# A decoder layer with a mixture of experts: the overflow turns run ahead of the last static expert, whose rows are added by 0/1 products on TensorE

## The reference, cut to what matters

```python
h2 = rms_norm(x, norm2_g) * (1 + sc2) + sh2
# 4 groups of 8 experts; per token: best group, then the best 2 experts in it, with gates
hg = einsum('nd,edf->nef', h2, w_gate)      # 32 experts, d = 1024, f = 128
hu = einsum('nd,edf->nef', h2, w_up)
act = silu(hg) * hu * gates
x = x + gt2 * einsum('nef,efd->nd', act, w_down)
out = rms_norm(x, final_g)
```

## Time and profile before

| | us |
|---|---|
| median of 3 runs | 873.32 |
| lowest, highest | 872.92, 874.47 |
| the profiled execution, its device time | 874.96 |
| the same execution, span of the profile | 873.2 |
| granted TensorE clock, mean of the span | 0.983 of full |
| PE busy | 815.8 |
| DVE busy | 460.3 |
| POOL busy | 278.8 |
| ACT busy | 240.4 |

### The profile page before, as it was taken

How to read it: one execution, slowest core, us unless ns; L and a number is a source line. 1 busy time by engine, 2 the same in 40 slices (tenths; PEclk the granted TensorE clock), 3 DMA queues, 4 the chain that set the end, 5 groups by cost and what they waited for, 6 DMA issues and landing times. The chain is left out here.

```text
span 873.2 us, 17369 instructions
## 1 busy us (share of the span) xinstructions
PE 815.8 (93%) x7175; PEld 544.7 (62%) x7175; DVE 460.3 (53%) x1154; ACT 240.4 (28%) x581; POOL 278.8 (32%) x267
## 2 busy tenths in 40 slices
PE   8999999999999999799888999999999999999950
PEld 8557544544444355777777455555788888888830
DVE  3750478887830136467664244434645555454534
ACT  6220111112200143455543112221233223232214
POOL 5810000000499501452741100000135565543332
PEclk9999999999999999999999999999999999999995
DMA  9934433445111123000000881112889989888639
GB/s 315 324 90 135 145 120 121 139 158 172 37 38 36 27 70 133 18 3 4 4 4 20 308 325 48 49 73 96 325 296 301 303 285 273 277 267 261 206 73 367
DMA packets 79719, 136.35 MB, mean 156 GB/s; under 512 B 17213, under 2 KB 51226, under 8 KB 79642
## 3 DMA queue, kind: packets, MB, share of 16 engines
q1 hardware_dynamic: 69338, 118.44, 39.0%
q0 software_dynamic: 10304, 16.82, 8.2%
HBM read 124.18 MB, written 29.92 MB: 176 GB/s over the span
## 5 line engine op out<-in xcount | busy, mean ns | idle before, releaser
L792 PE MATMUL banks<-REG_W 128*128 128x512 f32 (+2 forms) x832 | 274.6, 499 | 0.9 <-DVE pend L1988 0.5
L792 PEld LDWEIGHTS banks<-REG_W 128*128 128x128 f32 (+1 forms) x832 | 125.9, 182 | 135.3 <-issue 133.8
L792 PE MATMUL banks<-REG_W,REG_Y 128*128 128x512 f32 x256 | 118.3, 599 | 1.4 <-DVE REG_Y L2236 1.1
L1434 ACT ACTIVATE REG_P<-banks 128x256 f32<-128x256 f32 (+2 forms) x126 | 53.5, 463 | 156.8 <-PE banks L792 137.7
L792 PE MATMUL banks<-REG_P 64*64 64x64 f32 (+3 forms) x2752 | 79.5, 230 | 13.1 <-issue 8.9
L792 PEld LDWEIGHTS banks<-REG_P 64*64 64x64 f32 (+1 forms) x2752 | 67.6, 135 | 23.0 <-issue 16.4
L1434 ACT ACTIVATE REG_Y<-banks,mod,s 128x128 f32<-128x128 f32 x136 | 51.2, 457 | 85.8 <-PE banks L1386 85.8
L792 PEld LDWEIGHTS banks<-REG_W,REG_Y 128*128 128x128 f32 x256 | 45.6, 191 | 44.3 <-issue 44.2
L792 PEld LDWEIGHTS banks<-REG_Y,REG_P 128*128 128x128 f32 (+1 forms) x616 | 63.1, 181 | 7.0 <-issue 7.0
L792 PE MATMUL banks<-REG_Y,REG_P 128*128 128x128 f32 (+1 forms) x616 | 66.6, 276 | 0.1
L636 POOL TENSOR_TENSOR REG_P<-REG_P 128x1040 f32<-128x1040 f32 x2 | 4.8, 2390 | 175.8 <-DVE REG_P L1801 175.8
(11 more groups left out here) (295 smaller groups left out, 1108.1 us busy)
## 6 DMA issues: line engine op xcount, KB each, us to landing
REG_P<-in_w_ada SPq DMA_DIRECT2D x20, 1024.0 KB, 6.2
REG_W<-in_w_in SPq DMA_DIRECT2D x17, 512.0 KB
REG_P<-in_moe_w_gate SPq DMA_DIRECT2D x17, 512.0 KB, 8.3
REG_W<-in_moe_w_gate SPq DMA_DIRECT2D x16, 512.0 KB, 6.4
REG_W<-in_moe_w_up SPq DMA_DIRECT2D x16, 512.0 KB, 10.7
REG_W<-in_moe_w_down SPq DMA_DIRECT2D x16, 512.0 KB, 16.7
REG_P<-in_moe_w_up SPq DMA_DIRECT2D x14, 512.0 KB, 14.9
REG_P<-in_moe_w_down SPq DMA_DIRECT2D x12, 512.0 KB, 21.2
```

The costliest lines, as they stand in the source:

```text
L792: return pe.matmul(o_, l, r, start=start, stop=stop, skip_group_check=True)
L1434: return act.activation(o_, i_, f, **kw)
```

## The change

The last static expert (turn 31, `LAST`) is taken out of the static loop and put behind the overflow loop on PE, ACT and DVE. The overflow turns take the counts from LAST on, and scatter from buffer `yo[2]`. POOL scatters no rows for turn 31; it gathers tile E+1 ahead of the scatter of turn 30. DVE builds, between the result of turn 30 and the overflow loop, 8 matrices `hot[:, j]` of 0 and 1 (partition = place in the expert's list, column = token of tile j). SP loads `y_d` to `x1` when the last overflow scatter has landed, without turn 31. PE then makes `hot[:, j]` transposed times `yo`, two `mm` calls of 128x512 for each tile j, into a pair of PSUM banks, and DVE adds the pair to the loaded tile (`completed(j)`); ACT squares the tile behind that. `xg[3]` is set to zero by POOL once before its first gather.

```diff
--- before.py
+++ after.py
@@ -261,6 +261,9 @@
             rt[name], o = area(REG_P, o, *shape)
         assert o == RT + RT_LEN
         fsq, _ = area(REG_W, 0, 2, D)
+        hot, _ = area(REG_W, SLOT, NT, P)
+        LAST = E - 1
+        assert LAST % RING == 9 and LAST % RES == 1
 
 
         ident = sb("ident", [P, P])
@@ -367,7 +370,7 @@
                  "rt_pos  rt_hot far_ld rt_ld rt_n "
                  " m_tx m_xa m_xd m_gu m_th m_act m_dn m_yd "
                  "ov_w "
-                 "rt_c rt_e1 rt_e2 rt_oh f_go ov_go st_x1 f_ss f_o").split()
+                 "rt_c rt_e1 rt_e2 rt_oh ov_go st_x1 f_ss f_o").split()
         s = {n: sem(n) for n in names}
         s_ada = [sem(f"ld_ada{i}") for i in range(4)]
         s_win = [sem(f"ld_win{i}") for i in range(2)]
@@ -539,7 +542,7 @@
                 e = sp.value_load(eid_view(i), min_val=0, max_val=E - 1)
                 load_expert(0, e, s["ov_w"])
 
-            sp.wait_ge(s["f_go"], 1)
+            sp.wait_ge(s["ov_go"], n_ov + 1)
 
             for j in range(NT):
                 sp.dma_start(x1[:, j], y_d[j * P:(j + 1) * P, :]).then_inc(s_w[j], 16)
@@ -739,8 +742,9 @@
             for e in range(2):
                 gather(TURN[e], e)
             gp.wait_ge(s["st_x1"], 16 * NT)
-            for e in range(2, BUF):
-                gather(TURN[e], e)
+            gather(TURN[2], 2)
+            ch.step(gp.memset(xg[3], 0.0))
+            gather(TURN[3], 3)
 
             def gather_behind(e):
                 if e + BUF < E:
@@ -749,13 +753,13 @@
 
             for e in range(3):
                 gather_behind(e)
-            for e in range(E):
+            for e in range(LAST):
+                if e == LAST - 1:
+                    gp.wait_ge(s["m_tx"], E + 1)
+                    gather(E + 1, 0)
                 gp.wait_ge(s["m_yd"], e + 1)
                 scatter_add(rows_of(TURN[e], 0), e % RES)
                 gather_behind(e + 3)
-                if e == E - 1:
-                    gp.wait_ge(s["m_tx"], E + 1)
-                    gather(E + 1, 0)
                 if e + BUF == E:
                     gp.wait_ge(s["far_ld"], 32)
                     gp.wait_ge(s["m_tx"], E - BUF + 1)
@@ -769,16 +773,15 @@
                     gp.sem_inc(s["ov_go"], 1)
             n_ov = gp.value_load(idy[0:1, 0:1], min_val=1, max_val=OVT)
             for b in range(RES):
-                gp.wait_ge(s_sc[b], 16 * len(range(b, E, RES)))
+                gp.wait_ge(s_sc[b], 16 * len(range(b, LAST, RES)))
             with gp.Fori(0, n_ov) as i:
                 ch.enter(i, 4)
-                scatter_add(rows_of(i + E, 1, i + (E + 1)), 0)
+                scatter_add(rows_of(i + E, 1, i + E), 2)
                 gp.wait_ge(s_gx[0], i * 16 + 16 * (E // BUF + 2))
                 at = rows_of(i + (E + 2), 0, count=i + (E + 2), done="m_tx")
                 fetch(at, 0)
-                gp.wait_ge(s_sc[0], i * 16 + 16 * (len(range(0, E, RES)) + 1))
+                gp.wait_ge(s_sc[2], i * 16 + 16 * (len(range(2, LAST, RES)) + 1))
                 gp.sem_inc(s["ov_go"], 1)
-            gp.sem_inc(s["f_go"], 1)
 
             for i in range(NT // 2):
                 gp.wait_ge(s["f_ss"], i + 1)
@@ -1411,21 +1414,36 @@
             ex_t(1, 1, 16)
             ex_gu(0, 0, 0, wsem=s_w[0], wcount=w_loads(0, 1), wait_free=False)
 
-            for e in range(1, E):
-                if e + 1 < E:
-                    ex_t(e + 1, (e + 1) % BUF, 16 * ((e + 1) // BUF + 1))
+            for e in range(1, LAST):
+                ex_t(e + 1, (e + 1) % BUF, 16 * ((e + 1) // BUF + 1))
                 ex_gu(e, e % 2, e % RING, wsem=s_w[e % RING], wcount=w_loads(e % RING, e // RING + 1), wait_free=e >= 2)
                 ex_dn(e - 1, (e - 1) % 2, (e - 1) % RING, wait_free=e >= 3)
             ex_t(E, 0, 16 * (E // BUF + 1))
-            ex_dn(E - 1, (E - 1) % 2, (E - 1) % RING)
+            ex_dn(LAST - 1, 0, (LAST - 1) % RING)
 
             pe.wait_ge(s["rt_n"], 1)
             n_ov = pe.value_load(idy[0:1, 0:1], min_val=1, max_val=OVT)
             with pe.Fori(0, n_ov) as i:
                 ex_gu(i + E, 0, 0, "m_", s["ov_w"], i * 48 + 48, False)
-                pe.wait_ge(s["m_yd"], i + E)
-                ex_dn(i + E, 0, 0, "m_", False)
                 ex_t(i + (E + 1), 0, i * 16 + 16 * (E // BUF + 2))
+                pe.wait_ge(s["m_yd"], i + LAST)
+                ex_dn(i + LAST, 0, 0, "m_", False)
+
+            ex_gu(LAST, 1, LAST % RING, wsem=s_w[LAST % RING], wcount=w_loads(LAST % RING, LAST // RING + 1), wait_free=False)
+            ex_dn(n_ov + LAST, 1, LAST % RING, wait_free=False)
+            beside(8, 2)
+            for j in range(NT):
+                q = 2 * ((j + 1) % 4)
+                if j == 3:
+                    pe.wait_ge(s["m_xa"], n_ov + (E + 1))
+                    pe.wait_ge(s["m_xd"], n_ov + (E + 1))
+                if j >= 4:
+                    pe.wait_ge(s["op_x1"], NT + j - 3)
+                for h in range(2):
+                    if j == 0:
+                        pe.wait_ge(s["m_yd"], n_ov + (E + h))
+                    last = mm(PS[q + h][:, :], hot[:, j, :], yo[LAST % RES][:, h * 512:(h + 1) * 512])
+                last.then_inc(s["op_ps"], 1)
 
 
         @block.scalar
@@ -1670,20 +1688,20 @@
 
             act.wait_ge(s["op_ps"], NT)
             modulated(xt[:, 0], 0, 1, "m_tx", "m_xa", 0)
-            for e in range(E):
-                if e + 1 < E:
-                    modulated(xt[:, (e + 1) % 2], 0, e + 2, "m_tx", "m_xa", 0)
+            for e in range(LAST):
+                modulated(xt[:, (e + 1) % 2], 0, e + 2, "m_tx", "m_xa", 0)
                 hidden(e, e % 2, free=e >= 2)
             modulated(xt[:, 0], 0, E + 1, "m_tx", "m_xa", 0)
             act.wait_ge(s["rt_n"], 1)
             n_ov = act.value_load(idy[0:1, 0:1], min_val=1, max_val=OVT)
             with act.Fori(0, n_ov) as i:
-                hidden(i + E, 0, free=False)
+                hidden(i + LAST, 0, free=False)
                 modulated(xt[:, 0], 0, i + (E + 2), "m_tx", "m_xa", 0)
+            hidden(n_ov + LAST, 1, free=False)
 
 
             for j in range(NT):
-                act.wait_ge(s_w[j], w_loads(j, len(range(j, E, RING))) + 16)
+                act.wait_ge(s["op_x1"], NT + j + 1)
                 if j >= 2:
                     act.wait_ge(s["ss_ready"], 2 * NT + j - 1)
                 fn(fsq[:, j % 2], x1[:, j], ACT.Square, scale=ROOT, accum_out=ss[:, 2, j:j + 1]).then_inc(s["ss_ready"], 1)
@@ -2235,35 +2253,57 @@
                     dve.wait_ge(s[pre + "dn"], e - 1)
                 stt(ac[:, par, :], a1[:, par, :], 0.5, PS[2 + par][:, P:2 * P], ALU.mult, ALU.mult).then_inc(s[pre + "act"], 1)
 
+            def scaled_halves(b, par, by):
+                return [stt(yo[b][:, h * 512:(h + 1) * 512], PS[4 + 2 * par + h][:, :], by, gtb[:, 1, h * 512:(h + 1) * 512],
+                            ALU.mult, ALU.mult) for h in range(2)]
+
             def result(e, par, pre="m_"):
-                b = e % RES if isinstance(e, int) else 0
+                b = e % RES
                 dve.wait_ge(s[pre + "dn"], e + 1)
-                if isinstance(e, int) and e >= RES:
+                if e >= RES:
                     dve.wait_ge(s_sc[b], 16 * (e // RES))
-                for h in range(2):
-                    last = stt(yo[b][:, h * 512:(h + 1) * 512], PS[4 + 2 * par + h][:, :], gate(TURN[e] if isinstance(e, int) else e), gtb[:, 1, h * 512:(h + 1) * 512],
-                               ALU.mult, ALU.mult)
-                last.then_inc(s[pre + "yd"], 1)
+                scaled_halves(b, par, gate(TURN[e]))[1].then_inc(s[pre + "yd"], 1)
 
             modulated(xt[:, 0], 1, "m_tx", "m_xd", 1)
-            for e in range(E):
-                if e + 1 < E:
-                    modulated(xt[:, (e + 1) % 2], e + 2, "m_tx", "m_xd", 1)
+            for e in range(LAST):
+                modulated(xt[:, (e + 1) % 2], e + 2, "m_tx", "m_xd", 1)
                 hidden(e, e % 2, free=e >= 2)
                 if e == 3:
                     dve.wait_ge(s["st_x1"], 16 * NT)
                 if e >= 1:
                     result(e - 1, (e - 1) % 2)
             modulated(xt[:, 0], E + 1, "m_tx", "m_xd", 1)
-            result(E - 1, (E - 1) % 2)
+            result(LAST - 1, 0)
+
+            ch.step(dve.tensor_copy(gap[:, 0:1], tbl[:, TURN[LAST], 0:1]))
+            ch.step(stt(left[:, :], i32[:, 0:NT], -float(P), gap[:, 0:1].to_broadcast([P, NT]), ALU.mult, ALU.add))
+            for j in range(NT):
+                ts(hot[:, j, :].rearrange("p (a b) -> p a b", a=KD), i128[:, :].rearrange("p (b a) -> p a b", a=KD), left[:, j:j + 1], None, ALU.is_equal)
             dve.wait_ge(s["far_ld"], 32)
             n_ov = dve.value_load(idy[0:1, 0:1], min_val=1, max_val=OVT)
             with dve.Fori(0, n_ov) as i:
                 ch.enter(i, 1)
-                hidden(i + E, 0, free=False)
```

(30 more changed lines are left out.)

## The result

| | before | after |
|---|---|---|
| median of 5 runs, us | 872.92 | 880.55 |
| lowest, highest | 870.51, 874.47 | 878.46, 881.62 |
| profiled execution: device time, span | 874.96, 873.2 | 880.62, 878.2 |
| granted TensorE clock, mean of the span | 0.983 | 0.988 |
| PE busy, DVE busy, POOL busy | 815.8, 460.3, 278.8 | 831.7, 472.8, 275.2 |

The kernel is slower by 0.87% (ratio 1.0087, 95% interval 1.0065 to 1.011), which is 7.6 us; +7.1 was forecast.

The account below looks back on a forecast made before the run. From 826 us on it saw a chain of handovers, with DVE deciding the tail. Terms 0 + 1.0 + 0 + 6.1 = +7.1 us on the median 873.3 gave 880.4 us, range 876.5 to 886.0.

Parts of the forecast that it names:

- Part 1: Moving turn 31 behind the overflow turn: gains 0, as the overflow gather lands when it did; bounds -0.2 to +2.4 us.
- The feared loss: Next gather, issued later behind turn 29's scatter, could make the overflow's down product 2.4 us late; taken as 0.
- Part 2: PE's new idle stretch before the overflow transposes: granted clock falls and slows the work behind; +1.0 us, bounds 0 and 2.5.
- Part 3: Turn 31 and the 0/1 products on PE behind the overflow turn: just in time, pacing up to tile 3; 0 us.
- Part 4: DVE in the tail: four adds, roots and a stall move the last scaling's end by +6.1 us; bounds +4.8, +8.3.
- The roots: POOL's roots in the tail: 0.73 us beside adds, so no stall there; without the rule the forecast is 1.4 us later.
- Rival A: PE's wait for the overflow gather: the overflow turn moves forward up to 5.5 us, giving 873.9 us; chance 6%.
- Rival B: Clock stays at 0.50 through the overflow's products, which take 7.5 instead of 3.8 us, giving 885.6 us; chance 8%.
- Rival C: Tail: the loads are the chain, so DVE's four extra adds vanish in waits, giving 876.3 us; chance 5%.
- What it said would show it wrong: Signs against it: the overflow's products start before 833, or DVE has gaps over 2 us in the tail.
- the window of 849 to 852: Start of the tail: the first load of `y_d` was expected at 849 to 852 us.

Follow-up runs that it names:

- c2: Kernel before in its old order, with turn 31's rows added by the 0/1 products in the tail and not scattered: 879.07 us, ratio 1.0074.
- a3: Changed kernel with turn 31's gate and up products put back into PE's wait for the overflow gather: 879.27 us, ratio 1.0079.
- d1: Changed kernel with the overflow weights released after turn 23 and final_g loaded behind them, gathers unchanged: 880.75 us, ratio 1.0092.
- d2: d1 with 20 matmul calls (40 small matmuls) added in PE's wait for the overflow gather: 878.65 us, ratio 1.0059.
- a2: Changed kernel with DVE's adds of tiles 4 to 7 cut from 1024 to 128 columns: 878.51 us, ratio 1.006.
- a6: Changed kernel with root_args(3) moved between the two scalings of pair 2, so the last root runs beside a scaling: 879.37 us, ratio 1.0081.
- a7: Changed kernel with the edits of a5 and a6 together: 876.08 us, ratio 1.0045.
- a4: Changed kernel with both overflow gathers issued earlier, overflow weights as they are: 879.45 us, ratio 1.0075.
- a5: a4 with the overflow weights released after turn 23 instead of 27 and final_g loaded behind them: 876.29 us, ratio 1.0037.
- a1: Changed kernel with 40 small matmuls put into PE's wait for the overflow gather: 880.01 us, ratio 1.0071.

## Why the prediction was right, point by point

- **Part 1, value 0: held.** The transposes started 8.2 us behind the gather's issue, as before. The feared loss didn't come: the next gather, issued at 832.78, was there when PE came to its transposes at 838.34, at most 5.6 us later, and PE didn't stand in front of the overflow's down product at all. The compares on DVE ended with 0.1 us to spare, where 0.2 had been predicted. c2 and a3 show from both sides that nothing was to be gained here.
- **Part 2, +1.0: right kind, too small.** The fall before the landing and the return "some 2 to 5 us into the work" are as said; it came back at about 834. The term assumed that "the rest catches up" behind the transposes. It doesn't: turn 30's down product was slowed too (2.63 us after, 3.06 in d1, against 1.88), and nothing behind it had slack. The cost is 1.6 us by the mean of the fronts, 1.8 in d1 against d2.
- **Part 3, 0: held for the end, wrong in who paces.** Up to the end of the 16 small matmuls PE's times were within 0.6 us of those given. A tile of 0/1 products then takes 1.74 us (13.90 for eight) and not 1.88, so that tile 3 is done at about 856.7 and not 857.9. So PE doesn't set the pace up to tile 3: the loads do. All three of DVE's waits there are for `y_d`, and the add of tile 3 starts 8.4 us behind the first load, where 8.9 was predicted.
- **Part 4, +6.1: right, 1.0 too large.** The +6.1 is the move of the last scaling's end behind the first load; it measured 24.9 - 19.8 = +5.1. The add takes 1.22 us (1.2 taken). The stall in front of the last pair was 0.81, not 1.1; 0.5 us came from tile 3 starting earlier as above. Another 0.3 us, which the forecast put at nothing, lies between the last scaling and the end of the span (4.65 us after, 4.33 before), so that the tail measured +5.4. The listing of adds and scalings in DVE's order is what carried the forecast. What it left out is that the adds also cover the roots (a2), which doesn't change this sum but the price of one add.
- **The roots.** The traces show 0.73, 0.71 and 0.69 us for the three roots that run beside an add, with no wait in front of pairs 1 and 2, and 1.66 for the one that a6 and a7 put beside a scaling. By the Trainium skill, GPSIMD Engine Reference, Key points, POOL contends with DVE instructions that have two SBUF inputs; the scaling has two, the add takes one from PSUM. The traces agree, and the forecast without the rule would have been 1.4 us later.
- **The rivals.** Rival A needs both landings and was not there by itself (a4, a5). Rival B didn't happen after, but in part in a1 and a4, where PE waited directly in front of the overflow's products (5.47 instead of 3.8 us, where the rival had 7.5). Rival C, the adds hidden in waits, falls with the tail's +5.4.
- **What it said would show it wrong.** The overflow's products start at 834.77, behind the 833 named. DVE has one gap of 2.4 us, in front of the first add, where it waits for the first load; behind that none is over 1.2. By its letter ("gaps of more than 2 us in the tail") this sign was met, by a wait that stood there before in another form (10.28 us idle up to the first `root_args`) and says nothing against DVE as the bound behind it. The loads were issued at 848.70, 0.3 us ahead of the window of 849 to 852.

The two misses, +0.6 to +0.8 for the clock and -0.7 for the tail, cancel: the two causes and their order of size were forecast, but that the median (+7.6) lies closer to +7.1 than the parts do is luck.

## What to carry to other kernels

Before moving work out of a gap, ask what the gap waits for: here it was filled for free, and emptying it put nothing forward and let the clock fall. Taking a transfer off the path helps only if it was on it: turn 31's scatter lay hidden beside the overflow turn, and its replacement cost 5.4 us on the engine that was the bound of the last stretch, though that engine is busy for 54% of the whole. And where two landings lie close together, as the overflow's gather and its weights, one of them alone wins little: the front was 0.9 us shorter with the gather earlier (a4), not at all with the weights earlier (d1), and 4.5 us with both (a5).

## What the runs showed of the hardware that was not expected

- The same 128x2 root on POOL takes 0.70 us beside a DVE add with one PSUM input or beside nothing, and 1.66 us beside a DVE operation with two SBUF inputs: a factor of 2.4 for an instruction of 256 elements.
- 40 small identity matmuls in a wait of 5.6 us (5.55 in d1) held the clock at 1.00 through it (d2), at no cost, since PE still waited 1.00 us behind them.
- Weights issued 8.0 us earlier, measured from t0, landed 2.9 us earlier: the last matrix took 22.3 us from issue (a5) instead of 17.2.
- The clock can be low at another place than the one in question: in the profile after it is 0.83 over 450 to 460 us with PE busy for 8.08 of the 10 us; the kernel before shows 1.00 there with PE busy for 7.86. The code there is the same in both, and what made the difference is open. The stretch in the profile after, with the columns of the other stretches:

```profile
450.00:460.00 10.00, 8.08 (x314) 7.47 (x307) 2.62 (x7) 4.45 (x13) 9.72 (x8) 0.83 0.03 7
```
